# VectorE takes slot 0's logits ahead of the last index score, a weight split and a branch's low part; TensorE computes each slot's logits ahead of a value product

## The chip, the cores and the metric

One core of a Trainium2 chip runs the whole program. The metric is the device time of one execution in microseconds. The engines are TensorE (PE in the rows, PEld for its weight loads), VectorE (DVE), ScalarE (ACT), GpSimd (POOL) and SyncE (SP), whose queue loads the weights.

## The reference, cut to what matters

Two layers over 256 tokens of width 1024. Each has a gated feed-forward block, a mixer of three branches, a cross attention to a memory, and a second feed-forward block.

```python
for l in range(DEPTH):
    x = x + 0.5 * swiglu_ffn(rms_norm(x, ffn1_norm[l]), ffn1_w_gu[l], ffn1_w_down[l])
    h = rms_norm(x, mix_norm[l])
    (x_r, g_r, q_b, c_kv, q_i, k_i, w_i, q_c, k_c, v_c, f_c,
     gate_a, gate_b, gate_c) = jnp.split(h @ w_in[l], _split_points(), axis=-1)
    o_a = rglru_branch(x_r, g_r, ...)
    o_b = dsa_branch(q_b, c_kv, q_i, k_i, w_i, ...)
    o_c = fox_branch(q_c, k_c, v_c, f_c, forget_bias[l])
    merged = (jax.nn.sigmoid(gate_a) * (o_a @ w_branch[l, 0])
              + jax.nn.sigmoid(gate_b) * (o_b @ w_branch[l, 1])
              + jax.nn.sigmoid(gate_c) * (o_c @ w_branch[l, 2]))
    x = x + merged @ w_out[l]
    x = x + memory_cross_attention(...)
    x = x + 0.5 * swiglu_ffn(rms_norm(x, ffn2_norm[l]), ffn2_w_gu[l], ffn2_w_down[l])
```

Branch a is a gated linear recurrence. Branch c is causal attention with 8 heads of 64 and a bias that grows with distance (a cumulated forget gate). Branch b is attention over 64 selected keys per query; an index score chooses them: `score = einsum(relu(qi . ki), wi)` over 8 index heads, and the 64 largest of a row are kept.

## The kernel before, in words

**Units.** All weights stream through SBUF in units of 1 MB (`raw`, a ring of three slots). SyncE's queue loads a unit; ScalarE writes its rounded copy `w_hi` in two halves (L509); VectorE writes the remainder `w_lo = raw - w_hi` in two halves (L517). TensorE multiplies three times for each tile (hi by hi, hi by lo, lo by hi). The split of a unit into the two parts is made three units ahead: `splits(..., name)` splits the unit that follows `name` by three in the ring.

**The index stage.** Eight index slots (`for i in range(IDX_SLOTS)`): TensorE makes the dot products of two index heads, ScalarE takes their positive part into `lg[:, i % 2]` (L1005), and VectorE adds them to `score` with two multiply-adds (L1350, L1352), with the mask at every fourth slot. Behind every second slot stands one unit (`IDX_FILL`: qc0, kc0, qc1, kc1). VectorE also does the recurrence of branch a here, after slot 3. After slot 7 it makes `o_lo[0] = gr - o_hi[0]` (L1370), the low part of branch a's output, which unit ba0 reads in slot 6 of the stream, and then the split that belongs to `IDX_FILL[7]`.

**The stream.** Sixteen attention slots follow, `for s in range(STREAM + 3)`: slots 0 to 7 are branch c, 8 to 15 branch b; a slot is two heads of one block of 128 queries. The block is `(s % 8) // 4`, so slots 0 to 3 and 8 to 11 have 128 keys and the others 256. The work of one slot is spread over three turns of the loop, and each turn ends with one unit, `FILL[s]`: vc0, vc1, qb0, qb1, ga0, ga1, ba0, ga2, ga3, ba1, gc0, gc1, bc0, gc2, gc3, bc1, gb0, gb1, mk0. Each engine has this order written out by hand, and semaphores join them.

TensorE in turn s: transposes of the probabilities of slot s-1 (L1758, waits for GpSimd's `p_ready`); value product of slot s-2 (L1767, waits for the copy of the transposes and in slot 2 for the copies of vc0 and vc1); logits of slot s (L1779); `kb` in turns 2 and 3, `vb` in turn 8, four transposes of the memory in turns 13 to 16 (L1798); then the unit.

ScalarE in turn s: copy of the transposes of s-1 (L816), copy of the value product of s-2 (L1027), two half splits for `FILL[s-1]` (L509), exponentials of slot s (L1035, waits for VectorE's `lg_ready`), copies and gates of the unit (L816, L897).

VectorE in turn s: logits of s times scale plus bias and their minimum (L1386 and L1391, or L1395; L1398, `lg_ready`); the first half split for `FILL[s-1]` (L517; none in turn 0); reciprocal of the sums (L1403, waits for ScalarE's `exp_ready`); low part of the value product of s-2 (L1409); the second half split; in turns 0 to 7 two rounds of eight maxima of `score` (L1417, L1419); in turns with a unit ba, bc or bb, its merge with the gate (L1234, or L1238 and L1241), which frees the two PSUM halves that the unit used.

GpSimd in turn s: `lg` times the reciprocal (L777, `p_ready`), in turns 1 to 3 a mask (L731), from turn 7 on a bias with the mask for branch b (L743).

`Plan.mix` numbers the jobs in TensorE's order and hands out the four PSUM banks in turn; the logits have banks of their own (`acc_job`), so their place in the order moves no other job to another bank.

Of the kernel before, what the change touches and what calls it, by code (L numbers as in the profile page):

```python
# [21 lines left out]
F32 = mybir.dt.float32  # L22
F32R = mybir.dt.float32r
ACT = mybir.ActivationFunctionType
ALU = mybir.AluOpType
# [76 lines left out]
class Plan:  # L102
# [57 lines left out]
    def mix(self):  # L160
# [22 lines left out]
        for s in range(STREAM + 3):  # L183
            if 0 <= s - 1 < STREAM:
                self.job(("pt", s - 1))
            if 0 <= s - 2 < STREAM:
                self.job(("pv", s - 2))
            if s < STREAM:
                self.acc_job(("qk", s))
            if s in (2, 3):  # L190
                self.job(("kb", s - 2))
            if s == 8:
                self.job(("vb", 0))
                self.job(("vb", 1))
            if 13 <= s < 17:
                self.job(("mt", s - 13))
            self.w_unit(FILL[s])
# [46 lines left out]
def block_kernel(nc, t, out):  # L244

    ctx = ExitStack()
    with ctx:
# [880 lines left out]
        def _(v):  # L1128
# [127 lines left out]
            for l in range(DEPTH):  # L1256
# [83 lines left out]
                splits(v, split_lo, l, "qi1")  # L1340
                for i in range(IDX_SLOTS):
                    blk, h, base, m = idx_slot_of(i)
# [11 lines left out]
                    if i % 4 == 3:  # L1354
                        mask = chunked[:, SEQ - s_len:SEQ]
                        v.tensor_tensor(sc, sc, mask, ALU.add)
                        v.drain()
                    v.drain().then_inc(score_step, 1)
                    if i == 3:
                        v.wait_ge(rg_sqrt, l + 1)  # L1360
# [6 lines left out]
                        v.drain().then_inc(rg_h, 1)  # L1367
                    if i == 7:
                        v.wait_ge(oa_ready, l * 1 + 1)
                        v.tensor_tensor(o_lo[0][:], gr[:], o_hi[0][:].bitcast(F32), ALU.subtract)  # L1370
                        v.drain().then_inc(oa_lo_ready, 1)
                    if i in IDX_FILL:
                        splits(v, split_lo, l, IDX_FILL[i])

                for s in range(STREAM + 3):
                    if s < STREAM:
# [21 lines left out]
                        v.tensor_reduce(nm[:, s % 2, :], lgs, AX_X, ALU.min).then_inc(lg_ready, 1)  # L1398
                    if s >= 1:
                        splits(v, split_lo, l, FILL[s - 1], (0,))  # L1400
                    if s < STREAM:
                        v.wait_ge(exp_ready, l * STREAM + s + 1)
                        v.reciprocal(ri[:, s % 2, :], sm[:, s % 2, :]).then_inc(ri_ready, 1)  # L1403
                    if 0 <= s - 2 < STREAM:
# [5 lines left out]
                                        ALU.subtract).then_inc(bank_of(("pv", k)), 1)  # L1410
                    if s >= 1:
                        splits(v, split_lo, l, FILL[s - 1], (1,))
                    if s < 8:
# [79 lines left out]
        def _(pe):  # L1493
# [194 lines left out]
            for l in range(DEPTH):  # L1688
# [60 lines left out]
                for s in range(STREAM + 3):  # L1749
                    if 0 <= s - 1 < STREAM:  # L1750
# [4 lines left out]
                        for j in range(2):  # L1755
                            for c in range(n_s):
                                col = (j * n_s + c) * P
                                mm = pe.transpose(ps(("pt", k))[:, col:col + P], lg[:, k % 2, j, c * P:c * P + P], ident[:])  # L1758
                        mm.then_inc(job_done, 1)
                    if 0 <= s - 2 < STREAM:  # L1760
                        k = s - 2
# [3 lines left out]
                        for c in range(blk + 1):  # L1765
                            for j in range(2):
                                mm = pe.matmul(ps(("pv", k))[HD * j:HD * j + HD, 0:P],  # L1767
                                               values[:, c, (2 * pr + j) * HD:(2 * pr + j + 1) * HD],
                                               pt[:, k % 2, j, c, :], start=(c == 0), stop=(c == blk))
                        mm.then_inc(job_done, 1)  # L1770
                    if s < STREAM:
                        blk, pr = slot_of(s)
                        s_len = P * (blk + 1)
                        queries, keys = (qc, kc) if s < 8 else (qb, k_b)
                        wait_jobs(pe, l, [f"qc{pr // 2}", f"kc{pr // 2}"] if s < 8 else [f"qb{pr // 2}", ("kb", pr // 2)])
                        if s >= 2:
                            pe.wait_ge(lg_ready, l * STREAM + s - 1)
                        for j in range(2):
                            mm = pe.matmul(logits(s)[:, j, :], queries[HD * j:HD * j + HD, pr, blk * P:blk * P + P],  # L1779
                                           keys[HD * j:HD * j + HD, pr, 0:s_len], start=True, stop=True)  # L1780
                        mm.then_inc(job_done, 1)
# [86 lines left out]
```

## Time and profile before

| | us |
|---|---|
| median of 3 runs | 1404.04 |
| lowest, highest | 1403.73, 1405.26 |
| the profiled execution, its own time | 1402.98 |
| its span | 1401.1 |
| TensorE busy | 1359.5 (97%) |
| VectorE busy | 948.0 (68%) |
| ScalarE busy | 777.6 (56%) |
| GpSimd busy | 130.4 (9%) |

The span is the time from the first to the last instruction of the profiled execution. The share of busy time is a mean over all stages; the gaps of an engine are read in the timeline. The granted clock is 1.00 at 2.4 GHz and 0.50 at 1.2 GHz.

### The profile page before, as it was taken

To read this page: it belongs to the slowest core of one execution; us is meant where nothing else is said; L and a number is where in the kernel's file an instruction comes from. 1 tells how busy PE (TensorE), PEld (TensorE's weight loads), DVE (VectorE), ACT (ScalarE), POOL (GpSimd) and SP (SyncE) were. 2 spreads that over 40 slices of the span, in tenths; PEclk is the share of its full clock that TensorE was granted. 3 is DMA by queue.
4 is the path that set the end of the run, shared out by engine and by line. 5 is a ranking of instruction groups with operands and counts; after the bars stand their busy time and mean duration, and the time that the engine had idled before them with its cause. 6 is when DMAs were issued, how large, how long until landed. Compare 5 with 4: busy or idle time off the path is not lost.

```text
span 1401.1 us, 23740 instructions
## 1 busy us (share of the span) xinstructions
PE 1359.5 (97%) x8802; PEld 1211.1 (86%) x8802; DVE 948.0 (68%) x1456; ACT 777.6 (56%) x1378; POOL 130.4 (9%) x219
## 2 busy tenths in 40 slices
PE   6999999999999999999999999999999999999997
PEld 5888879988899988888888888898989989888886
DVE  5666656879666566666676666668777666666665
ACT  5554545845654565554565555576546446655544
POOL 4010000022320110000010000000224001100000
PEclk9999999999999999999999999999999999999999
DMA  8677664544545546666666667456344554466662
GB/s 241 187 209 210 186 194 151 170 136 154 174 136 185 191 121 181 188 196 187 179 182 194 194 180 213 138 169 191 121 156 146 163 198 151 140 191 186 198 186 75
DMA packets 286384, 243.38 MB, mean 174 GB/s; under 512 B 14344, under 2 KB 263608, under 8 KB 286304
## 3 DMA queue, kind: packets, MB, share of 16 engines
q1 hardware_dynamic: 284176, 236.77, 55.9%
q10 hardware_dynamic: 1600, 4.25, 0.9%
q0 software_dynamic: 528, 1.26, 0.5%
q8 instruction: 54, 0.88, 0.3%
q14 instruction: 26, 0.21, 0.0%
HBM read 241.18 MB, written 1.27 MB: 173 GB/s over the span
## 4 chain that ended last, share of the span: by engine, by line
issue 64%; PE 23%; ACT 4%; DVE 3%; POOL 2%; DVEq 2%; POOLq 1%; DMA 1%; ACTq 0%
PE work L1550 14%; PE work L1625 2%; PE work L1572 2%; ACT w_hi L509 1%; PE acc L1587 1%; PE work L1629 1%; DVE w_lo L517 1%; POOL diag L723 1%; PE acc L1501 1%; PE acc L1779 1%; DVE score L1352 1%; POOLq L722 1%; PE work L1767 1%; ACT lg L1035 1%; DVEq L1353 1%
## 5 line engine op out<-in xcount | busy, mean ns | idle before, releaser
L517 DVE TENSOR_TENSOR w_lo<-raw,w_hi 128x1024 fp32r<-128x1024 f32 x444 | 552.8, 1265 | 100.2 <-ACT w_hi L509 98.7
L509 ACT ACTIVATE w_hi<-raw 128x1024 fp32r<-128x1024 f32 (+1 forms) x442 | 450.9, 1053 | 24.5 <-PE acc L1587 24.5
L1625 PE MATMUL work<-act,w_hi 128*128 128x512 f32 x1408 | 441.4, 395 | 9.8 <-DVE w_lo L517 5.8
L1629 PEld LDWEIGHTS work<-act,w_lo 128*128 128x128 f32 x1408 | 265.5, 189 | 60.5
L1550 PE MATMUL work<-act,w_hi 128*128 128x256 f32 x1664 | 299.1, 281 | 5.3 <-DVE merged L1241 2.5
L1629 PE MATMUL work<-act,w_lo 128*128 128x256 f32 x1408 | 278.4, 279 | 0.0
L1550 PEld LDWEIGHTS work<-act,w_hi 128*128 128x128 f32 x1664 | 255.3, 188 | 13.4 <-issue 5.4
L1550 PE MATMUL work<-act,w_lo 128*128 128x256 f32 x832 | 230.7, 277 | 0.0
L1625 PEld LDWEIGHTS work<-act,w_hi 128*128 128x128 f32 x1408 | 215.4, 188 | 13.6 <-issue 10.6
L823 ACT ACTIVATE gu_s<-work 128x256 f32<-128x256 f32 x176 | 57.9, 381 | 200.8 <-PE work L1629 200.8
L1550 PEld LDWEIGHTS work<-act,w_lo 128*128 128x128 f32 x832 | 156.3, 188 | 0.6 <-issue 0.5
L1161 DVE TENSOR_TENSOR gu_s<-gu_s,work 128x256 f32<-128x256 f32 x176 | 66.2, 418 | 130.1 <-ACT gu_s L823 130.1
L1587 PE MATMUL acc<-w_hi,h_lo 128*128 128x512 f32 x320 | 126.0, 394 | 0.0
L1587 PE MATMUL acc<-w_lo,h_hi 128*128 128x512 f32 x320 | 125.4, 392 | 0.0
L1587 PE MATMUL acc<-w_hi,h_hi 128*128 128x512 f32 x320 | 124.2, 388 | 0.0
L833 ACT ACTIVATE h_hi<-h_f 128x256 fp32r<-128x256 f32 x80 | 33.4, 418 | 102.2 <-PE acc L1587 86.4
L714 POOL TENSOR_TENSOR ms<-ssq 128x1 f32<-128x1 f32 x22 | 5.2, 235 | 878.3 <-ACT junk L798 878.3
L1587 PEld LDWEIGHTS acc<-w_lo,h_hi 128*128 128x128 f32 x320 | 60.1, 188 | 12.3
L1587 PEld LDWEIGHTS acc<-w_hi,h_lo 128*128 128x128 f32 x320 | 60.2, 188 | 11.9
L1587 PEld LDWEIGHTS acc<-w_hi,h_hi 128*128 128x128 f32 x320 | 60.1, 188 | 11.8
L1180 DVE TENSOR_TENSOR h_lo<-h_f,h_hi 128x256 fp32r<-128x256 f32 x80 | 33.8, 423 | 49.2 <-ACT h_hi L833 49.2
L1550 PE MATMUL work<-o_hi,w_hi 128*128 128x256 f32 x192 | 53.8, 280 | 0.0
(240 smaller groups left out, 1726.8 us busy)
## 6 DMA issues: line engine op xcount, KB each, us to landing
raw<-in_ffn_w_gu SPq DMA_DIRECT2D x174, 512.0 KB, 5.0
raw<-in_w_in SPq DMA_DIRECT2D x52, 1024.0 KB, 5.2
raw<-in_ffn_w_down SPq DMA_DIRECT2D x44, 1024.0 KB, 4.9
raw<-in_w_branch SPq DMA_DIRECT2D x12, 1024.0 KB, 5.0
raw<-in_w_mkv SPq DMA_DIRECT2D x8, 1024.0 KB, 5.3
raw<-in_w_out SPq DMA_DIRECT2D x8, 1024.0 KB, 4.9
raw<-in_w_mq SPq DMA_DIRECT2D x4, 1024.0 KB, 5.2
raw<-in_w_mo SPq DMA_DIRECT2D x4, 1024.0 KB, 4.9
```

Of the source, the lines that this page charges most:

```text
L509: eng.activation(halves(w_hi, slot, kind, part), halves(raw, slot, kind, part), ACT.Copy)\
L517: eng.tensor_tensor(halves(w_lo, slot, kind, part), halves(raw, slot, kind, part), halves(w_hi, slot, kind, part).bitcast(F32), ALU.subtra ...
L722: g.drain()
L823: a.activation(gu_s[:, c, g, :], work[:, 2 * c + g, SEQ:2 * SEQ], ACT.Copy).then_inc(cross_ready, 1)
L833: a.activation(dst[:, c, :], h_f[:, c, :], ACT.Copy).then_inc(h_hi_ready, 1)
L1161: v.tensor_tensor(gu_s[:, c, g, :], gu_s[:, c, g, :], work[:, 2 * c + g, 0:SEQ], ALU.add)\
L1180: v.tensor_tensor(lo[:, c, :], h_f[:, c, :], hi[:, c, :].bitcast(F32), ALU.subtract)\
L1550: mm = pe.matmul(out_ps, ww[:, slot, first:first + width], xx[:, k, :], start=(k == 0 and n == 0), stop=(k == kn - 1 and n == 2))
L1572: mm = pe.matmul(out_ps(tt), xx[:, k, tt * P:tt * P + P], ww[:, slot, k * 256 + cols[0]:k * 256 + cols[1]], start=(k == 0 and n == 0), sto ...
L1587: mm = pe.matmul(acc[:, tt, nh * 512:nh * 512 + 512], xx[:, k0 + kk, tt * P:tt * P + P], ww[:, slot, kk * D + nh * 512:kk * D + nh * 512 + ...
L1625: pe.matmul(work[:, 2 * c + g, :], w_hi[:, slot, at_w:at_w + P], act[:, :, k, :], start=(k == 0), stop=False, skip_group_check=True)
L1629: mm = pe.matmul(work[:, 2 * c + g, 0:SEQ], w_lo[:, slot, at_w:at_w + P], act_hi[:, k, :], start=False, stop=(k == KT - 1), skip_group_che ...
```

## The change

On VectorE the last index score (slot 7) goes behind the logits and the minimum of slot 0 of the stream. The split that stood behind it goes into turn 0 in two halves: one ahead of the reciprocal of slot 0, one behind it. The low part of branch a's output goes behind the second half. On TensorE the logits of slot s go ahead of the value product of slot s-2 in every turn. ScalarE and GpSimd keep their order, and so do the loads.

```diff
@@ Plan.mix
             if 0 <= s - 1 < STREAM:
                 self.job(("pt", s - 1))
+            if s < STREAM:
+                self.acc_job(("qk", s))
             if 0 <= s - 2 < STREAM:
                 self.job(("pv", s - 2))
-            if s < STREAM:
-                self.acc_job(("qk", s))
@@ vector
-                for i in range(IDX_SLOTS):
+                def index_scores(i):
                     blk, h, base, m = idx_slot_of(i)
...
+                for i in range(IDX_SLOTS - 1):
+                    index_scores(i)
                     if i == 3:
...
-                    if i == 7:
-                        v.wait_ge(oa_ready, l * 1 + 1)
-                        v.tensor_tensor(o_lo[0][:], gr[:], o_hi[0][:].bitcast(F32), ALU.subtract)
-                        v.drain().then_inc(oa_lo_ready, 1)
                     if i in IDX_FILL:
                         splits(v, split_lo, l, IDX_FILL[i])
...
-                    if s >= 1:
-                        splits(v, split_lo, l, FILL[s - 1], (0,))
+                    if s == 0:
+                        index_scores(IDX_SLOTS - 1)
+                    ahead = FILL[s - 1] if s else IDX_FILL[IDX_SLOTS - 1]
+                    splits(v, split_lo, l, ahead, (0,))
                     if s < STREAM:
                         v.wait_ge(exp_ready, l * STREAM + s + 1)
                         v.reciprocal(ri[:, s % 2, :], sm[:, s % 2, :]).then_inc(ri_ready, 1)
...
-                    if s >= 1:
-                        splits(v, split_lo, l, FILL[s - 1], (1,))
+                    splits(v, split_lo, l, ahead, (1,))
+                    if s == 0:
+                        v.wait_ge(oa_ready, l * 1 + 1)
+                        v.tensor_tensor(o_lo[0][:], gr[:], o_hi[0][:].bitcast(F32), ALU.subtract)
+                        v.drain().then_inc(oa_lo_ready, 1)
@@ tensor
                         mm.then_inc(job_done, 1)
+                    if s < STREAM:
+                        blk, pr = slot_of(s)
+                        s_len = P * (blk + 1)
+                        queries, keys = (qc, kc) if s < 8 else (qb, k_b)
+                        wait_jobs(pe, l, [f"qc{pr // 2}", f"kc{pr // 2}"] if s < 8 else [f"qb{pr // 2}", ("kb", pr // 2)])
+                        if s >= 2:
+                            pe.wait_ge(lg_ready, l * STREAM + s - 1)
+                        for j in range(2):
+                            mm = pe.matmul(logits(s)[:, j, :], queries[HD * j:HD * j + HD, pr, blk * P:blk * P + P],
+                                           keys[HD * j:HD * j + HD, pr, 0:s_len], start=True, stop=True)
+                        mm.then_inc(job_done, 1)
                     if 0 <= s - 2 < STREAM:
                         k = s - 2
                         blk, pr = slot_of(k)
...
-                        mm.then_inc(job_done, 1)
-                    if s < STREAM:
-                        blk, pr = slot_of(s)
-                        s_len = P * (blk + 1)
-                        queries, keys = (qc, kc) if s < 8 else (qb, k_b)
...
```

VectorE, from index slot 6 to slot 0's maxima, before (`score` is the index score, `w_lo` a weight split, `o_lo` the low part, `lg` and `nm` slot 0's logits and their minimum; x4 are slots 6 and 7 together):

```order
L1352 SCALAR_TENSOR_TENSOR score<-lg,wi,score 128x256 x4
L1356 TENSOR_TENSOR score<-score,chunked 128x256
L1370 TENSOR_TENSOR o_lo_70<-gr,o_hi_69 128x1024
L517 TENSOR_TENSOR w_lo<-raw,w_hi 128x1024 x2
L1386 SCALAR_TENSOR_TENSOR lg<-acc,fox_bias 128x2x128
L1391 TENSOR_TENSOR lg<-lg,causal 128x2x128
L1398 TENSOR_REDUCE nm<-lg 128x2
L1403 RECIPROCAL ri<-sm 128x2
```

The same place in the changed kernel:

```order
L1352 SCALAR_TENSOR_TENSOR score<-lg,wi,score 128x256 x2
L1385 SCALAR_TENSOR_TENSOR lg<-acc,fox_bias 128x2x128
L1390 TENSOR_TENSOR lg<-lg,causal 128x2x128
L1397 TENSOR_REDUCE nm<-lg 128x2
L1352 SCALAR_TENSOR_TENSOR score<-lg,wi,score 128x256 x2
L1356 TENSOR_TENSOR score<-score,chunked 128x256
L517 TENSOR_TENSOR w_lo<-raw,w_hi 128x1024
L1404 RECIPROCAL ri<-sm 128x2
L517 TENSOR_TENSOR w_lo<-raw,w_hi 128x1024
L1415 TENSOR_TENSOR o_lo_70<-gr,o_hi_69 128x1024
```

The logits moved ahead of slot 7's scores; the split is in two pieces around the reciprocal, and the low part stands behind them, ahead of the maxima.

TensorE at the head of turn 6, before: transposes of slot 5, the value product of slot 4 (`pt,vc`), the logits of slot 6 (`kc,qc`), then the first product of unit ba0.

```order
L1758 MATMUL work<-ident,lg 128x128 x4
L1767 MATMUL work<-pt,vc 64x128 x4
L1779 MATMUL acc<-kc,qc 128x256 x2
L1550 MATMUL work<-o_hi_69,w_hi 128x256
```

The same place in the changed kernel:

```order
L1762 MATMUL work<-ident,lg 128x128 x4
L1772 MATMUL acc<-kc,qc 128x256 x2
L1782 MATMUL work<-pt,vc 64x128 x4
L1554 MATMUL work<-o_hi_69,w_hi 128x256
```

The value product and the logits have changed places; what stands ahead of and behind the two is as before.

## Rows read from the trace of the kernel before

**Rows 1.** Waits of TensorE: line, for whom, us in total, times, longest.

```profile
PE work L1758 <- POOL lg L777: 5.6, 2, 2.8
...
PE work L1550 <- DVE merged L1241: 2.5, 4, 0.6
```

**Rows 2.** Windows, TensorE: us, busy (count), granted clock, DMA share, GB/s.

```profile
292.50:295.90 3.40, 3.40 (x18) 0.50 0.00 1
978.60:985.40 6.80, 6.32 (x29) 0.50 0.30 98
```

**Rows 3.** Timeline, TensorE, layer 0: start, us, engine, line, operation, [idle before].

```profile
282.41 0.39 PE L1572 MATMUL work<-w_hi,act 128*128 128x256 f32 x1
...
288.05 0.28 PE L1572 MATMUL work<-w_hi,act 128*128 128x256 f32 x1
291.13 0.44 PE L1758 MATMUL work<-ident,lg 128*128 128x128 f32 x2 [2.80 <-POOL lg L777]
291.50 0.49 PE L1779 MATMUL acc<-kc,qc 64*128 64x128 f32 x4
...
299.21 0.38 PE L1758 MATMUL work<-ident,lg 128*128 128x128 f32 x2
300.14 0.44 PE L1767 MATMUL work<-pt,vc 128*64 128x128 f32 x4 [0.56 <-ACT vc L816]
```

**Rows 4.** Timeline, TensorE, layer 1, slots 0 and 1.

```profile
979.08 0.69 PE L1758 MATMUL work<-ident,lg 128*128 128x128 f32 x2 [2.77 <-POOL lg L777]
...
988.40 0.38 PE L1758 MATMUL work<-ident,lg 128*128 128x128 f32 x2
```

**Rows 5.** Timeline, VectorE, layer 0, slots 0 and 1.

```profile
282.51 1.05 DVE L1352 SCALAR_TENSOR_TENSOR score<-lg,wi,score 128x256 f32<-128x256 f32 x2 [0.17 <-issue]
...
284.22 1.23 DVE L1370 TENSOR_TENSOR o_lo<-gr,o_hi 128x1024 fp32r<-128x1024 f32 x1 [0.17 <-issue]
285.57 2.36 DVE L517 TENSOR_TENSOR w_lo<-raw,w_hi 128x1024 fp32r<-128x1024 f32 x2
287.85 0.42 DVE L1386 SCALAR_TENSOR_TENSOR lg<-acc,fox_bias 128x256 f32<-128x256 f32 x1
...
290.22 0.17 DVE L1403 RECIPROCAL ri<-sm 128x2 f32<-128x2 f32 x1 [0.95 <-ACT lg L1035]
...
292.04 0.42 DVE L1386 SCALAR_TENSOR_TENSOR lg<-acc,fox_bias 128x256 f32<-128x256 f32 x1 [0.24 <-PE acc L1779]
```

**Rows 6.** Timeline, ScalarE, layer 0, slot 0.

```profile
284.60 1.28 ACT L1035 ACT_TABLE_LOAD   x1
289.31 0.40 ACT L1035 ACTIVATE lg<-lg,nm 128x128 f32<-128x128 f32 x1 [3.42 <-DVE nm L1398]
```

**Rows 7.** Timeline, GpSimd beside VectorE, layer 0.

```profile
259.38 1.36 POOL L731 TENSOR_TENSOR fox_bias<-fox_bias,causal 128x256 f32<-128x256 f32 x1 [16.06 <-DMA fox_bias<-cum_dram]
...
260.06 2.90 DVE L517 TENSOR_TENSOR w_lo<-raw,w_hi 128x1024 fp32r<-128x1024 f32 x2
...
294.68 0.17 DVE L1403 RECIPROCAL ri<-sm 128x2 f32<-128x2 f32 x1
...
294.92 1.51 POOL L777 TENSOR_TENSOR lg<-lg,ri 128x256 f32<-128x256 f32 x1 [3.85 <-DVE ri L1403]
```

**Rows 8.** Timeline, three engines, layer 0, slots 6 and 7.

```profile
329.40 0.66 PE L1767 MATMUL work<-pt,vc 128*64 128x128 f32 x8
...
329.98 0.70 PE L1779 MATMUL acc<-kc,qc 64*128 64x256 f32 x4
...
330.10 0.28 ACT L1027 ACTIVATE o_hi<-work 128x128 fp32r<-128x128 f32 x1
...
332.22 0.51 ACT L1035 ACTIVATE lg<-lg,nm 128x256 f32<-128x256 f32 x1
...
337.81 1.29 DVE L1234 SCALAR_TENSOR_TENSOR merged<-gate,work 128x512 f32<-128x512 f32 x2
...
338.56 0.39 PE L1550 MATMUL work<-act,w_hi 128*128 128x256 f32 x1 [0.54 <-DVE merged L1234]
```

More of the change, by code:

```diff
@@ L1769, in _ @@
                                                pt[:, k % 2, j, c, :], start=(c == 0), stop=(c == blk))
-                        mm.then_inc(job_done, 1)
-                    if s < STREAM:
-                        blk, pr = slot_of(s)
-                        s_len = P * (blk + 1)
-                        queries, keys = (qc, kc) if s < 8 else (qb, k_b)
[L1775 to L1780, printed above, removed]
                         mm.then_inc(job_done, 1)
```

## The prediction

> **What bounds the kernel now.** I read the waits of TensorE first: the engine is busy nearly throughout, so only its gaps and its clock can give time back. Two kinds of wait matter here. Both waits for GpSimd's normalised probabilities (5.6 us, two times) stand ahead of slot 0's transposes, once per layer, and four waits of about 0.6 us are for a merge by VectorE [rows 1]. Then I read the granted clock: after the first of the long waits it is 0.50 for the whole of 292.5 to 295.9, and around the second it is 0.50 from 978.6 to 985.4 [rows 2]. So a long wait costs its own length and a stretch at 1.2 instead of 2.4 GHz behind it.
>
> TensorE's rows in layer 0: unit vc0 runs from 282.41 to 288.05 + 0.28 = 288.33, that is 5.92 us; the transposes of slot 0 start at 291.13 after 2.80 us idle; those of slot 1 at 299.21; the value product of slot 0 at 300.14 waits 0.56 us for ScalarE's copy of vc1 [rows 3]. From slot 0's transposes to slot 1's it takes 8.08 us there, and 988.40 - 979.08 = 9.32 us in layer 1 [rows 3, 4]. At the full clock it would be 0.37 (transposes to logits, 291.13 to 291.50) + 0.42 (the logits; their row has 0.49, its end modelled) + 5.92 = 6.71 us. The low clock therefore costs 1.37 us in layer 0 and 2.61 us in layer 1.
>
> Why slot 0 is late is in VectorE's rows: slot 0's logits are ready when vc0 starts (282.41), but VectorE does the last index score at 282.51, the branch's low part at 284.22, both halves of a weight split at 285.57 and only at 287.85 the logits; the reciprocal comes at 290.22 [rows 3, 5]. Nothing waits for the three pieces ahead of it at that moment.
>
> **The change, part by part.**
>
> *Slot 0 on VectorE.* No instruction is added or removed. The step 282.51 is now slot 0's logits, say 282.55. ScalarE's exponentials begin as the minimum is there, 289.31 - 287.85 = 1.46 us after the logits' start [rows 5, 6], so the minimum is at 284.01, and VectorE itself is free at about 283.95. Then the last index score takes 284.22 - 282.51 = 1.71 us, to 285.66, and half of the pair of splits (287.85 - 285.57) / 2 = 1.14 us, to 286.80 [rows 5]. ScalarE is not ready at 284.01: its table load runs from 284.60 to 285.88 [rows 6]. The exponentials then need 290.22 - 289.31 = 0.91 us to the reciprocal [rows 5, 6]: 286.79. Both arms meet, and the reciprocal is at 286.80.
>
> Behind it VectorE starts the other half split at once. This is how slot 1 runs now: reciprocal at 294.68, GpSimd's product from 294.92 and 1.51 us long, so 1.75 us from reciprocal to probabilities [rows 7]. I take 1.75 us: 288.55, and the transposes at 288.61. TensorE arrives at 288.33. The stall falls from 2.80 to 0.28 us in layer 0 and, the rows of layer 1 having the same shape (2.77 [rows 4]), to about 0.27 there: 2.52 + 2.50 = 5.02 us. The low clock behind the stall should go too: 1.37 + 2.61 = 3.98 us. That takes a gap of 0.3 us as harmless, as those of 0.56 us [rows 3] are.
>
> The Trainium skill, page "SBUF — State Buffer", section "Who interferes with whom", speaks against this placing: a VectorE instruction with both inputs in SBUF and a GpSimd instruction that reads SBUF exclude each other, and the one issued second waits for the whole of the first. The 1.51 us row agrees with it; were there no such exclusion, the sum would be at most 0.28 us per layer better, 6.7 us and not 6.1.
>
> *Slot 1 pays for it.* The low part (1.35 us from 284.22 to 285.57, with its drain [rows 5]) now stands behind the second half split: 286.88 + 1.14 = 288.02. GpSimd's product slips between the two: at 259.38 a GpSimd instruction lasted 1.36 us between two long ones of VectorE and the pair of splits behind took 2.90 us and not 2.36 [rows 5, 7], so VectorE waits 0.54 us. The low part ends at 289.9. The two rounds of maxima run from 290.30 (0.08 behind the reciprocal) to 292.04 - 0.24 = 291.80 now [rows 5], 1.50 us: so slot 1's logits start at 291.4 and not 292.04, 0.64 us earlier, while TensorE is 2.5 us earlier. Reciprocal 2.64 us later (294.68 - 292.04, partly ScalarE's), then 1.75 us: probabilities at 295.8. TensorE arrives at 288.61 + 6.71 = 295.32. That is 0.5 us; where ScalarE is not in the way it is 0.3. I take 0.4 us a layer: -0.8 us.
>
> *Logits ahead of the value product, slot 2.* The 0.56 us wait at 300.14 [rows 3] is covered by slot 2's logits (0.42) and by the stall just counted: +0.56 twice, 1.12 us.
>
> *The same exchange in the other slots.* VectorE gets its logits 0.4 to 0.6 us earlier, but the value product ends later by the logits' length, and ScalarE copies that product before it does two half splits, and only then the exponentials. Slot 6 shows it: value product 329.40, logits 329.98 with 0.70, ScalarE's copy at 330.10, then without a gap the splits and the exponentials at 332.22 [rows 8]. With the logits first the value product starts about 0.6 us later, the copy too, and the exponentials, and VectorE cannot take its reciprocal before. In most slots this is hidden: probabilities are ready ahead of TensorE (slot 1 now: 294.92 + 1.51 = 296.43 against 299.21, of which 1.37 is the slow clock, so 1.4 us in hand [rows 3, 7]). But behind slot 6 VectorE goes without a pause to the merge at 337.81, and TensorE's next unit waits for it, 0.54 us at 338.56 [rows 8]. That wait grows by 0.6 us. The other merges that TensorE waits for are those of bc0 and bc1 (slots 12 and 15), the four waits in [rows 1]. Slot 15 has slot 6's shape: 0.6 us. In slot 12 the value product is half as long and ScalarE is itself late: between 0 and 0.6, I choose 0.4. Together 1.6 us a layer, -3.2 us; the bounds are 0 (the earlier logits make up for it) and 0.7 (the logits' whole row) at each of six places, 4.2 us.
>
> **Sum.** 5.02 + 3.98 - 0.8 + 1.12 - 3.2 = 6.1 us gained. The profiled execution took 1402.98 us (span 1401.1), 1.06 us less than the median of the runs, 1404.04. From the median: 1397.9, say 1398.0 us. Weight loads should follow: a split moves by under 1 us, and its unit is used two units of 6 us later.
>
> **Rivals.**
> 1. The exchange is free, as the earlier logits let VectorE catch up at the merges: 9.3 us gained, 1394.7. For it: VectorE waits for logits in many slots. Against: the exponentials follow ScalarE's splits in slot 6 [rows 8]. Chance 0.2.
> 2. GpSimd does not get in between the split and the low part, and waits for both: probabilities 1.14 to 1.35 us later, of which slot 1's 0.4 comes back; 0.8 us a layer, 1399.6. For it: VectorE's next long instruction is there at once. Against: the row at 259.38 [rows 7]. Were the clock to fall again as well, 0.5 us would be left. Chance 0.08.
> 3. The longer stalls at the merges bring the clock down there: 1.37 to 2.61 us each, one a layer, 4 us: 1402. For it: at bc1's merge two waits lie close together. Against: single gaps of 0.54 and 0.56 us do not do it. Chance 0.12.
> 4. Slower: ScalarE's lateness of 0.5 us reaches the transposes in all of slots 3 to 15, and not only three merges: 13 x 0.5 x 2 = 13 us against 9.3 gained, 1407.7. It decides where probabilities are less than 0.6 us ahead of TensorE; slot 1 has 1.4 us. Chance 0.05.
> 5. The edit at slot 0 does nothing: another wait, ScalarE's table load or GpSimd, holds the transposes as long; then only 1.12 - 3.2, that is 1406.1. Chance 0.03.
>
> The forecast has 0.52. **Range and chances.** 1393.0 (rival 1, with slot 1's stall gone too) to 1402.0 (rival 3) leaves rivals 4 and 5 and the tails out. About 0.2% (2.8 us) is what a measurement of this kernel can tell from no change: faster is below 1401.2, slower above 1406.8. Faster: 0.52, 0.2, 0.08 and a third of rival 3: 0.84. Within: most of rivals 3 and 5: 0.11. Slower: rival 4: 0.05.
>
> **What the changed kernel's profile would show.** TensorE waits under 0.6 us for slot 0's transposes, and the granted clock stays at its upper level there. The reciprocal of slot 0 is about 3.4 us earlier against unit vc0, GpSimd's product there lasts about 1.5 us, and slot 1's transposes wait some 0.4 us. The wait for vc1's copy is gone. The waits for merges go from about 0.6 to about 1.1 us in both layers; if they stay at 0.6 or vanish, my price of the exchange was wrong. I am wrong altogether if transposes in slots 2 to 15 wait, or if slot 0's wait stays over 2 us.

## The result and the profile after

The changed kernel takes 1395.74 us (median of 6 runs, 1393.06 to 1397.28) and the kernel before 1404.19 us (6 runs, 1402.01 to 1405.26). The ratio is 0.9944, 95% interval 0.9934 to 0.9954: 7.9 us less, 6.5 to 9.3. The forecast was 6.1 us less. Timed once more in a later series (below), the same kernel came to 0.9969 (0.9956 to 0.9982), 4.4 us less. The two intervals do not overlap, so a difference of 2 us between two kernels of this case is taken as shown only with a trace behind it. The profiled execution of the changed kernel took 1396.78 us (span 1394.9), that of the kernel before 1402.98.

The waits of TensorE in the changed kernel, which answer to [rows 1] (line, for whom, us in total, times, longest):

```profile
PE work L1554 <- DVE merged L1234: 2.2, 2, 1.1
...
PE work L1802 <- DVE merged L1241: 1.5, 2, 0.7
PE work L1554 <- DVE merged L1241: 1.3, 2, 0.6
PE work L1762 <- POOL lg L777: 1.2, 4, 0.3
```

The wait for GpSimd's probabilities fell from 5.6 us in two pieces to 1.2 us in four; the waits for merges grew. The windows around slot 0's transposes, which answer to [rows 2] (us, busy, granted clock, DMA share, GB/s):

```profile
288.20:291.00 2.80, 2.54 (x20) 1.00 0.63 174
291.00:296.00 5.00, 4.68 (x40) 1.00 0.32 112
974.70:982.00 7.30, 6.78 (x55) 1.00 0.47 144
```

The granted clock is 1.00 behind both, where it was 0.50 for 3.4 us and for 6.8 us. VectorE's timeline in slots 0 and 1, layer 0, which answers to [rows 5]:

```profile
282.35 0.42 DVE L1385 SCALAR_TENSOR_TENSOR lg<-acc,fox_bias 128x256 f32<-128x256 f32 x1 [0.39 <-PE acc L1772]
...
286.64 0.17 DVE L1404 RECIPROCAL ri<-sm 128x2 f32<-128x2 f32 x1
286.73 1.21 DVE L517 TENSOR_TENSOR w_lo<-raw,w_hi 128x1024 fp32r<-128x1024 f32 x1
287.85 1.63 DVE L1415 TENSOR_TENSOR o_lo<-gr,o_hi 128x1024 fp32r<-128x1024 f32 x1
...
291.22 0.42 DVE L1385 SCALAR_TENSOR_TENSOR lg<-acc,fox_bias 128x256 f32<-128x256 f32 x1
```

GpSimd beside it, which answers to [rows 7]:

```profile
286.89 1.52 POOL L777 TENSOR_TENSOR lg<-lg,ri 128x256 f32<-128x256 f32 x1 [26.51 <-DVE ri L1404]
```

The reciprocal is 4.29 us after the logits' start, and the probabilities are ready at 288.41. The low part lasts 1.63 us and not 1.23: GpSimd's product got in ahead of it. TensorE in the same stretch and behind slots 6 and 15, which answers to [rows 3, 8]:

```profile
288.46 0.44 PE L1762 MATMUL work<-ident,lg 128*128 128x128 f32 x2 [0.30 <-POOL lg L777]
...
295.49 0.44 PE L1762 MATMUL work<-ident,lg 128*128 128x128 f32 x2 [0.32 <-POOL lg L777]
...
335.04 0.39 PE L1554 MATMUL work<-act,w_hi 128*128 128x256 f32 x1 [1.12 <-DVE merged L1234]
...
402.31 0.63 PE L1802 MATMUL work<-ident,mem_x 128*128 128x128 f32 x4 [0.74 <-DVE merged L1241]
403.58 0.38 PE L1554 MATMUL work<-act,w_hi 128*128 128x256 f32 x1 [0.65 <-DVE merged L1241]
```

Slot 2's wait for vc1's copy is gone, the wait behind slot 6 went from 0.54 to 1.12 us, and there is none behind slot 12. From slot 0's to slot 1's transposes it is 7.03 us (8.08 and 9.32 before). Why the merges are late shows in three engines in slot 6 (start, us, engine):

```profile
325.94 0.66 PE L1782 MATMUL work<-pt,vc 128*64 128x128 f32 x8
...
326.64 0.28 ACT L1027 ACTIVATE o_hi<-work 128x128 fp32r<-128x128 f32 x1 [0.58 <-PE work L1782]
...
328.71 0.50 ACT L1035 ACTIVATE lg<-lg,nm 128x256 f32<-128x256 f32 x1
...
334.30 1.28 DVE L1234 SCALAR_TENSOR_TENSOR merged<-gate,work 128x512 f32<-128x512 f32 x2
```

ScalarE now stands 0.58 us for the value product, where it went on without a gap before [rows 8]; in VectorE's rows of the same slot the reciprocal now waits 0.27 us for the exponentials, where it did not wait before.

### The profile page after: what moved, and what is told of

It reads as the page before. It is cut to its first block, busy times and chain, and to the rows that moved or that the text cites. A ratio compares the mean times of both kernels' runs of the same rounds, so it can differ in the third digit from the quotient of the medians.

```text
span 1394.9 us, 23740 instructions
## 1 busy us (share of the span) xinstructions
PE 1357.8 (97%) x8802; PEld 1208.2 (87%) x8802; DVE 945.5 (68%) x1456; ACT 780.3 (56%) x1378; POOL 134.6 (10%) x219
## 4 chain that ended last, share of the span: by engine, by line
issue 63%; PE 27%; ACT 3%; DVE 2%; POOL 2%; POOLq 1%; DMA 1%; DVEq 0%; ACTq 0%; SPq 0%
PE work L1554 17%; PE work L1629 3%; PE work L1633 1%; PE acc L1591 1%; PE acc L1772 1%; ACT w_hi L509 1%; PE work L1782 1%; PE work L1576 1%; POOL diag L723 1%; PE work L1762 1%; DVE w_lo L517 1%; PE acc L1505 1%; PE work L1748 0%; POOLq L722 0%; DMA rows_dram<-brow_dram 0%
## 5 line engine op out<-in xcount | busy, mean ns | idle before, releaser
L777 POOL TENSOR_TENSOR lg<-lg,ri 128x256 f32<-128x256 f32 (+1 forms) x32 | 36.7, 1147 | 200.2 <-DVE ri L1404 200.2
```

The costliest lines, as they stand in the source:

```text
L777: g.tensor_tensor(lg[:, s % 2, :, 0:s_len], lg[:, s % 2, :, 0:s_len], ri[:, s % 2, :].unsqueeze(2).to_broadcast([P, 2, s_len]), ALU.mult)\
```

## The experiments

The theory in test has three parts: VectorE's edit carries the whole gain, by a shorter stall and by the clock; the exchange on TensorE costs through ScalarE's queue; and slot 1 pays a little for the low part. The rivals: the exchange carries part of the gain; VectorE's own work makes the merges late. Ratios are to runs of the kernel before beside them. The table's first row is a series of its own; rows 2 to 5, rows 6 to 8 and rows 9 to 12 are three more, each on one chip.

| kernel | median us | ratio | 95% interval |
|---|---|---|---|
| changed kernel | 1395.74 | 0.9944 | 0.9934 to 0.9954 |
| VectorE's edit alone | 1395.48 | 0.9946 | 0.9932 to 0.9960 |
| exchange alone | 1407.42 | 1.0025 | 1.0013 to 1.0036 |
| low part in turn 2 | 1397.29 | 0.9956 | 0.9942 to 0.9970 |
| no exchange in turns 6, 15 | 1396.46 | 0.9953 | 0.9939 to 0.9967 |
| ScalarE's split first | 1392.99 | 0.9923 | 0.9906 to 0.9940 |
| low part in turn 2, exchange in turn 2 alone | 1393.78 | 0.9931 | 0.9914 to 0.9947 |
| low part ahead of the reciprocal | 1400.58 | 0.9978 | 0.9968 to 0.9989 |
| changed kernel again | 1398.03 | 0.9969 | 0.9956 to 0.9982 |
| split first, low part in turn 2 | 1393.17 | 0.9929 | 0.9912 to 0.9945 |
| the same without the exchange | 1394.84 | 0.9938 | 0.9922 to 0.9954 |
| exchange alone again | 1406.26 | 1.0023 | 1.0013 to 1.0034 |

### VectorE's edit alone

```diff
@@ against the changed kernel: Plan.mix, and the same two blocks on TensorE
-            if s < STREAM:
-                self.acc_job(("qk", s))
             if 0 <= s - 2 < STREAM:
                 self.job(("pv", s - 2))
+            if s < STREAM:
+                self.acc_job(("qk", s))
```

> Only VectorE's edit is made; TensorE keeps the value product ahead of the logits. My theory: the whole gain of the change is VectorE's edit, the exchange is a small net loss. The stall ahead of slot 0's transposes is 0.3 us, that of slot 1 0.3 us, slot 2's value product waits 0.2 to 0.6 us for vc1's copy, and the waits for merges are those of the kernel before (0.54, 0.6, 0.25 + 0.65 us a layer). No low clock at slot 0. 8.5 us less than before, that is as fast as the changed kernel or up to 1 us faster. Rival (the exchange carries part of the gain): 5 to 7 us less than before.

0.9946, 7.6 us less (5.6 to 9.5). The same gain as the whole change within the interval. TensorE's timeline of this kernel in layer 0:

```profile
288.26 0.44 PE L1762 MATMUL work<-ident,lg 128*128 128x128 f32 x2 [0.30 <-POOL lg L777]
...
295.29 0.44 PE L1762 MATMUL work<-ident,lg 128*128 128x128 f32 x2 [0.53 <-POOL lg L777]
...
334.27 0.39 PE L1554 MATMUL work<-act,w_hi 128*128 128x256 f32 x1 [0.55 <-DVE merged L1234]
...
401.33 0.63 PE L1802 MATMUL work<-ident,mem_x 128*128 128x128 f32 x4 [0.25 <-DVE merged L1241]
```

The merge waits of this layer are those of the kernel before, to 0.01 us; in layer 1 the one behind slot 12 is 0.42 us, as in the second trace of the kernel before. Slot 1's transposes wait 0.53 us here and 0.33 us in layer 1. Slot 2's value product does not wait in this trace, where I had 0.2 to 0.6 us: slot 1's own wait covers vc1's copy. The interval of the time reaches into the rival's 5 to 7 us; what speaks against the rival is the exchange alone, next.

### The exchange alone, twice

```diff
@@ against the kernel before: Plan.mix, and the same two blocks on TensorE
+            if s < STREAM:
+                self.acc_job(("qk", s))
             if 0 <= s - 2 < STREAM:
                 self.job(("pv", s - 2))
-            if s < STREAM:
-                self.acc_job(("qk", s))
```

> Only the exchange on TensorE is made; VectorE keeps its order. My theory: slot 0 still stalls 2.8 us with the low clock behind it; slot 2's wait of 0.56 us goes, slot 6's merge wait grows from 0.54 to 1.1 us, slot 15's from 0.25 + 0.65 to 0.75 + 0.65 us, slot 12's goes either way. Within 1.5 us of the kernel before. Rival (the exchange is a gain): 2 us or more less than before.

1.0025, 3.5 us slower (1.8 to 5.1), where I had within 1.5. The profiled execution was one of the quickest, 1402.89 us: the low clock is missing at layer 0's slot 0, and the merge waits are 1.13 us behind slot 6 in layer 0 alone, none behind slot 12, and 0.75 + 0.64 us behind slot 15, 3.9 us in all against 4.1 in the kernel before. So it was run again:

> The exchange alone once more, since it came out 3.5 us slower than the kernel before where its trace showed no such loss. Theory (the waits at the merges grow by 0.6 and 0.5 us and the one behind slot 12 goes either way; the speed of the pairs and the clock belong to the single execution): 0 to 2 us more than the kernel before. Rival (the exchange alone brings the slow pairs or the low clock more often): 3 to 4 us more again.

1.0023 again, 3.2 us: outside the theory's 0 to 2, and the rival's size. TensorE's waits in the second trace of it:

```profile
PE work L1758 <- POOL lg L777: 5.5, 2, 2.8
...
PE work L1550 <- DVE merged L1241: 2.6, 4, 0.6
PE work L1550 <- DVE merged L1234: 2.2, 2, 1.1
PE work L1798 <- DVE merged L1241: 2.2, 4, 0.7
```

and in the second trace of the kernel before, of the same form:

```profile
PE work L1758 <- POOL lg L777: 5.5, 2, 2.8
...
PE work L1550 <- DVE merged L1241: 2.1, 4, 0.6
PE work L1767 <- ACT vc L816: 1.1, 2, 0.6
PE work L1550 <- DVE merged L1234: 1.1, 2, 0.5
...
PE work L1798 <- DVE merged L1241: 0.5, 2, 0.2
```

Merges and vc1's copy together are 7.0 us against 4.8: the exchange loses 2.2 us in waits, the forecast's own price for it (3.2 lost, 1.1 gained). Some 1 us of the measured 3.4 (the mean of the two) is not in these waits and stays open. The rival's cause, a low clock more often, may be part of it in the second series and is not in the first: the mean granted clock of the runs was 0.9925 against 0.9924 of the kernel before in the first series, and 0.9911 against 0.9926 in the second.

### The low part in turn 2

```diff
-                    if s == 0:
+                    if s == 2:
                         v.wait_ge(oa_ready, l * 1 + 1)
                         v.tensor_tensor(o_lo[0][:], gr[:], o_hi[0][:].bitcast(F32), ALU.subtract)
```

> The changed kernel with the low part of branch a in turn 2 of the stream in place of turn 0. My theory: slot 1's transposes no longer wait (0.32 us a layer in the changed kernel), slot 0's wait stays 0.3 us; slot 2's wait for vc1's copy comes back in part (0.1 to 0.2 us). 0.3 to 0.7 us less than the changed kernel. Rival (GpSimd, which had the low part in its way, is the one that gains): slot 0's wait falls too.

In the trace slot 1's transposes do not wait any more and slot 0's wait is 0.30 us, as the theory has it; nothing waits in slot 2 either, where I had 0.1 to 0.2 us. The time does not show the 0.6 us: 0.9956 lies between the two results of the changed kernel.

In layer 0 of this trace the wait behind slot 6 is gone too; in layer 1 it is 1.12 us. What differs ahead of the two merges is above all who got in first, GpSimd's product or VectorE's half split; layer 0, then layer 1:

```profile
329.84 2.14 POOL L777 TENSOR_TENSOR lg<-lg,ri 128x512 f32<-128x512 f32 x1 [5.41 <-DVE ri L1404]
329.86 1.22 DVE L517 TENSOR_TENSOR w_lo<-raw,w_hi 128x1024 fp32r<-128x1024 f32 x1
...
1015.22 1.04 POOL L777 TENSOR_TENSOR lg<-lg,ri 128x512 f32<-128x512 f32 x1 [6.29 <-DVE ri L1404]
1015.25 2.10 DVE L517 TENSOR_TENSOR w_lo<-raw,w_hi 128x1024 fp32r<-128x1024 f32 x1
```

The second run of the changed kernel, below, comes back to this.

### No exchange in turns 6 and 15

```diff
+def logits_first(s):
+
+    return s not in (6, 15)
...
+                    for kind in ("qk", "pv") if logits_first(s) else ("pv", "qk"):
```

> The changed kernel with the logits ahead of the value product in all turns but 6 and 15. My theory (the exchange makes ScalarE's copy, splits and exponentials late, and with them VectorE's merge): the wait behind slot 6 falls from 1.12 to 0.5 to 1.0 us (turns 4 and 5 still carry part of the lateness), that behind slot 15 from 0.74 to 0.25 us; 1.0 to 2.1 us less than the changed kernel. Rival (VectorE's own work makes the merge late): both waits stay.

Waits of this kernel in layer 0:

```profile
335.24 0.39 PE L1560 MATMUL work<-act,w_hi 128*128 128x256 f32 x1 [0.88 <-DVE merged L1240]
...
378.86 0.63 PE L1809 MATMUL work<-ident,mem_x 128*128 128x128 f32 x4 [0.34 <-DVE merged L1247]
380.13 0.38 PE L1560 MATMUL work<-act,w_hi 128*128 128x256 f32 x1 [0.64 <-DVE merged L1247]
...
402.54 0.63 PE L1809 MATMUL work<-ident,mem_x 128*128 128x128 f32 x4 [0.25 <-DVE merged L1247]
```

Behind slot 15 the wait is back at 0.25 us and behind slot 6 it fell to 0.88, in both layers, both inside the theory's values: the exchange made them. That the 0.34 us left behind slot 6 come from the turns ahead of it is argued, not shown. Behind slot 12 0.34 + 0.64 = 0.98 us came up, which the first trace of the changed kernel did not have. The time (0.9953) shows no gain over the changed kernel's first result, where I had 1.0 to 2.1 us; against its second, whose trace has the same 0.98 us, it is 2.2 us less.

### ScalarE's half split ahead of its copy

```diff
@@ scalar
+                    if s >= 1:
+                        splits(a, split_hi, l, FILL[s - 1], (0,))
                     if 0 <= s - 2 < STREAM:
                         k = s - 2
                         blk, pr = slot_of(k)
                         wait_done(a, l, ("pv", k))
...
                     if s >= 1:
-                        splits(a, split_hi, l, FILL[s - 1])
+                        splits(a, split_hi, l, FILL[s - 1], (1,))
```

> The changed kernel, but ScalarE does the first half split of a turn ahead of its copy of the value product and the second behind it, so that it no longer stands idle for the product that now ends later. My theory (the merge waits grew because ScalarE stood behind the later value product): the wait behind slot 6 falls from 1.12 to about 0.5 us and that behind slot 15 from 0.74 to 0.25 us in both layers, with the logits still first everywhere. Rival (VectorE's own work, or the earlier logits, makes the merges late): they stay at 1.1 and 0.74. By the time: 1 to 2 us less than the changed kernel, which its own spread may hide.

ScalarE's copy of the value product in slot 6, and TensorE's waits, in layer 0, with the logits first in every turn:

```profile
326.25 0.28 ACT L1029 ACTIVATE o_hi<-work 128x128 fp32r<-128x128 f32 x1
...
333.70 0.39 PE L1556 MATMUL work<-act,w_hi 128*128 128x256 f32 x1 [0.42 <-DVE merged L1236]
...
400.70 0.63 PE L1804 MATMUL work<-ident,mem_x 128*128 128x128 f32 x4 [0.17 <-DVE merged L1243]
```

The copy does not wait any more (0.58 us in the changed kernel). The waits are 0.42 and 0.17 us in both layers, against 1.12 and 0.74 in the changed kernel and 0.54 and 0.25 before. Behind slots 6 and 15 GpSimd gets in first here as in the changed kernel's first trace, so that is not what changed. Taking ScalarE's wait for the value product away is enough: that wait was the cause, and the rival falls, since VectorE's work is unchanged. Now the earlier logits even gain 0.1 us at each of these two places; behind slot 12 the wait is 0.61 us. 0.9923: 10.8 us less than the kernel before, and 3 or 6.5 us less than the two results of the changed kernel, where I had 1 to 2: more than the waits of the traces account for. It is the best version by its ratio; the interval clears that of the second timing of the changed kernel and overlaps that of the first.

### One exchange only

```diff
+    return s == 2
...
-                    if s == 0:
+                    if s == 2:
                         v.wait_ge(oa_ready, l * 1 + 1)
```

> VectorE's edit with the low part in turn 2, and the logits ahead of the value product in turn 2 alone. My theory: every stall has its smallest value at once: slot 0 at 0.3 us, slots 1 and 2 none, merges 0.54, 0 or 0.6, and 0.25 + 0.65 us. 1 us less than VectorE's edit alone. Rival (the low part in turn 2 delays slot 2's chain): a wait at slot 2's transposes.

0.9931. Slot 0 waits 0.31 us, slots 1 and 2 not at all, and the merges 0.55, 0.42, 0.25 and 0.65 us. The theory's waits, to 0.2 us. It is 2.1 us below VectorE's edit alone (0.9946), where I had 1; the two intervals overlap, so that difference is not shown.

### The low part ahead of the reciprocal

```diff
                     splits(v, split_lo, l, ahead, (0,))
+                    if s == 0:
+                        v.wait_ge(oa_ready, l * 1 + 1)
+                        v.tensor_tensor(o_lo[0][:], gr[:], o_hi[0][:].bitcast(F32), ALU.subtract)
+                        v.drain().then_inc(oa_lo_ready, 1)
                     if s < STREAM:
                         v.wait_ge(exp_ready, l * STREAM + s + 1)
...
-                    if s == 0:
-                        v.wait_ge(oa_ready, l * 1 + 1)
-                        v.tensor_tensor(o_lo[0][:], gr[:], o_hi[0][:].bitcast(F32), ALU.subtract)
-                        v.drain().then_inc(oa_lo_ready, 1)
```

> The changed kernel with the low part ahead of slot 0's reciprocal, which makes the stall ahead of slot 0's transposes longer by its 1.35 us: 1.6 us where the kernel before had 2.8 and the changed one has 0.3; slot 1 should not wait. It asks from which length on a stall brings the clock down. Theory A (the clock falls with the long stalls only): no low clock at slot 0, 2.0 to 2.7 us more than the changed kernel. Rival B (1.6 us is long enough): the granted clock is 0.50 behind it for 3.4 us or more, 5 to 8 us more than the changed kernel.

The stall, and the windows behind it in both layers:

```profile
289.20 0.44 PE L1762 MATMUL work<-ident,lg 128*128 128x128 f32 x2 [1.55 <-POOL lg L777]
...
295.75 0.38 PE L1762 MATMUL work<-ident,lg 128*128 128x128 f32 x2
```

```profile
289.20:296.00 6.80, 6.80 (x56) 1.00 0.53 166
976.80:983.00 6.20, 6.20 (x52) 1.00 0.65 179
```

The clock stayed up behind 1.55 and 1.52 us in this execution, which is theory A, and slot 1 does not wait. The time decides less: by the ratios it is 4.8 us above the changed kernel's first result and 1.3 us above its second, where A had 2.0 to 2.7 and B 5 to 8. The mean granted clock of its 12 runs is 0.9942, against 0.9965 and 0.9953 in the two series of the changed kernel and 0.9914 in the kernel before beside it; so the clock may fall at slot 0 in some of its other executions, which no trace shows.

### The kernel before, again

No edit.

> The kernel before once more, for a second trace of it. In its first trace the stretch from the last merge wait to the third transposes (406.9 to 477.2, and 1096.5 to 1166.8) took 70.3 us in both layers, while four other kernels with the same instructions there took 72.0 us in most layers. If the speed of TensorE's pairs there belongs to the single execution, 72.0 us can come up here too; if the exchange makes it slow, it is 70.3 us again in both layers. The stalls at slot 0 are 2.8 us again.

72.0 us came up, in the very kernel that had 70.3: TensorE's windows from 410 to 470, first of this trace, then of the first trace of the kernel before (us, busy, matmuls, granted clock):

```profile
410.00:470.00 60.00, 60.00 (x420) 1.00 0.54 180
```

```profile
410.00:470.00 60.00, 60.00 (x434) 1.00 0.56 189
```

420 and 434 matmuls in 60 us, the same instructions at the same granted clock. The whole stretch has 516 matmul records in either trace, in 72.0 and in 70.3 us, so it is not a matter of missing records. In the 14 traces of this case, two stretches each, it took 70.3 us 7 times and 72.0 us 21 times, and the 70.3 came up with and without the exchange. So this belongs to the execution; why is open. The stalls at slot 0 were 2.78 and 2.76 us again.

### The changed kernel, again

No edit.

> The changed kernel once more, timed beside its variants on one chip, and with a second trace. Theory: 0.993 to 0.996 of the kernel before. Stalls as in its first trace: 0.3 us at slots 0 and 1, 1.12 us behind slot 6, 0.74 + 0.65 us behind slot 15; behind slot 12 it is 0 or about 1 us, as GpSimd or VectorE gets in first there.

0.9969. Behind slot 12 it waits 0.34 + 0.64 us this time. What differs stands in slot 12, GpSimd's product beside VectorE's half split; first trace, then the second:

```profile
374.71 2.14 POOL L777 TENSOR_TENSOR lg<-lg,ri 128x512 f32<-128x512 f32 x1 [4.25 <-DVE ri L1404]
374.73 1.22 DVE L517 TENSOR_TENSOR w_lo<-raw,w_hi 128x1024 fp32r<-128x1024 f32 x1
```

```profile
374.60 1.04 POOL L777 TENSOR_TENSOR lg<-lg,ri 128x512 f32<-128x512 f32 x1 [4.14 <-DVE ri L1404]
374.62 2.10 DVE L517 TENSOR_TENSOR w_lo<-raw,w_hi 128x1024 fp32r<-128x1024 f32 x1
```

Both start 0.02 us apart. In the first, GpSimd takes 1.1 us longer and VectorE goes on at once, so the merge is early; in the second VectorE stands 0.9 us. In slot 15 of the second trace it went in VectorE's favour in both layers and left only 0.62 us of wait there.

In the slots ahead of the three merges it is the exchange that opens this. Slots 6, 12 and 15 of both layers in the 14 traces are 84 such pairs. In 54 of them VectorE stood less than 0.6 us for the exponentials ahead of its reciprocal, and GpSimd got in first every time; all 30 pairs of the five traces without the exchange in these slots (the kernel before twice, VectorE's edit alone, one exchange only, the split first without the exchange) are among them. In the other 30, all with the exchange, VectorE stood 0.70 us, and it got in first in 12: there the merge wait is gone behind slots 6 and 12, and 0.62 us behind slot 15. So ScalarE's lateness costs a longer wait or, by chance, takes one away.

### Split first, with and without the exchange

```diff
@@ both, against the variant with ScalarE's split first
-                    if s == 0:
+                    if s == 2:
                         v.wait_ge(oa_ready, l * 1 + 1)
@@ the second alone: Plan.mix, and the same two blocks on TensorE
-            if s < STREAM:
-                self.acc_job(("qk", s))
             if 0 <= s - 2 < STREAM:
                 self.job(("pv", s - 2))
+            if s < STREAM:
+                self.acc_job(("qk", s))
```

> The changed kernel with ScalarE's first half split ahead of its copy of the value product, and the low part in turn 2. Theory: as the variant with the split first (stalls of 0.4, 0.6 and 0.2 + 0.6 us at the merges), and slot 1's wait of 0.31 us gone: 0.6 us less than that variant, about 0.992 of the kernel before. Rival: slot 2's chain, now behind the low part, waits and gives it back.

> VectorE's edit with the low part in turn 2 and ScalarE's first half split ahead of its copy, but the value product ahead of the logits as in the kernel before. It asks whether the exchange is worth anything once ScalarE does not wait for it. Theory: merge waits as in the kernel before (0.54, 0.6 or 0, 0.25 + 0.65 us), slot 2's value product waits about 0.5 us for vc1's copy. 0.5 to 1.5 us more than the same with the logits first. Rival (the exchange is worth nothing or costs): the same time or less.

0.9929 with the exchange and 0.9938 without. The first has no wait in slots 1 and 2; the second waits 0.56 us in slot 2 for vc1's copy in both layers. That is 1.1 us in the traces and 1.7 us in the medians, inside the intervals, so the worth of the exchange here is shown by the waits and not by the time. The first is not faster than the split alone (0.9923), where I had 0.6 us less: slot 1's wait is under what can be measured.

## Why the prediction was right, and where it was not

**Slot 0.** The forecast had the reciprocal at 286.80 and a stall of 0.28 us; the trace has 286.64 and 0.30. Both arms met there as worked out: VectorE's half split ended at 286.61, and ScalarE's last row of exponentials too, its table load having ended at 285.71. GpSimd's product lasted 1.52 us, as in [rows 7]. In slot 2 of the same trace the same pair went the other way:

```profile
299.98 0.61 POOL L777 TENSOR_TENSOR lg<-lg,ri 128x256 f32<-128x256 f32 x1 [3.86 <-DVE ri L1404]
300.00 1.67 DVE L517 TENSOR_TENSOR w_lo<-raw,w_hi 128x1024 fp32r<-128x1024 f32 x1
```

The rule of the Trainium skill, page "SBUF — State Buffer", section "Who interferes with whom", agrees with both placings: whichever of the two gets in first holds the other up. Behind the half split the product took 1.52 us and not 0.61; behind the product the half split took 1.67 us and not 1.21.

**The clock.** No low clock at slot 0 in any of the ten traces with VectorE's edit; in the four traces without it (the kernel before twice, the exchange twice) it was 0.50 in one layer at least. The price of 3.98 us holds for the first trace of the kernel before. It differs between places and executions: with stalls of 2.8 us the low stretch was 3.4 us at one place and 6.8 at another, and in the second trace of the same kernel it took 8.09 us from slot 0's to slot 1's transposes in both layers, not 8.08 and 9.32. Over all runs the mean granted clock lies between 0.9942 and 0.9970 in the ten series with VectorE's edit, and between 0.9911 and 0.9926 in the two of the exchange alone and the three of the kernel before beside them, so the gain in clock is not one of single executions. (For the kernel before in the first series the clock of each run is not known.)

**Slot 1.** 0.32 us against 0.4. The variant with the low part ahead of the reciprocal, where slot 1 does not wait, has 295.75 - 289.20 = 6.55 us from slot 0's to slot 1's transposes at the full clock. The forecast's 6.71 was built from rows whose ends are modelled and is 0.16 us too long: the low clock cost 0.16 us a layer more than I had, and slot 1's wait costs 0.48 us by the time and not 0.32. The two cancel in the sum.

**Slot 2.** The wait went, 0.56 us a layer. VectorE's edit alone did the same in both layers, by slot 1's own wait; the exchange earns it only where slot 1 does not wait, as the last pair of variants shows.

**The exchange elsewhere.** Behind slot 6 it went from 0.54 to 1.12 us (forecast 1.14), behind slot 15 from 0.25 to 0.74 (0.85). ScalarE's queue is shown as the cause by moving one half split. In slot 12 I chose a growth of 0.4 us, and the wait vanished in the first trace and was 0.98 us (forecast 1.01) in the second: what I did not see is that two engines start there 0.02 us apart, and that the exchange makes either of them come first. This term, 2 x 1.0 us, is what was mis-sized in the first trace: 1.2 us saved in place of 0.8 lost. In the second trace it was slot 15 that gained: 0.62 us of wait, where 0.90 had been and 1.50 was forecast.

**The sum.** Forecast 6.1 us less; measured 7.9 and 4.4, a mean of 6.2. The waits in the first pair of traces: 2.50 - 0.32 + 0.56 - 0.58 + 0.61 - 0.49 = 2.28 us a layer, 4.6 for both, and 4.0 for the clock: 8.5 in all. Its profiled execution is only 6.2 us shorter: 1.7 us went back where layer 0's stretch of 70.3 us took 72.0, and the remaining 0.6 us in smaller pieces that I did not follow. The second traces of both kernels, summed the same way, give 4.94 (slot 0's stall), 2.12 (from slot 0's to slot 1's transposes, clock and slot 1's wait together), 1.12 (slot 2), -1.15, -1.12 and +0.54 (slots 6, 12 and 15): 6.45 us, where the two executions are 8.0 apart. So the mechanism and the terms are borne out, but that the mean of two timings falls on the forecast to 0.1 us is luck: the two are 3.5 us apart, and who gets in first, the speed of the stretch and the low clock elsewhere each move an execution by 1 us or more. The range's lower end was also added up wrong: rival 1 with slot 1's stall gone is 1393.9, not 1393.0.

Rival 1 (the exchange is free) is out: it costs 2.2 us in waits and 3.4 us by the time when alone. Rival 2 (GpSimd overtaken twice) is out by the low part's 1.63 us. Rival 3 (the clock falls at the merges) showed in no trace. Rival 4 (slower) is out: no transposes in slots 2 to 15 wait in either trace of the changed kernel. Rival 5 (no effect at slot 0) is out by the stall of 0.30 us.

## What to carry to other kernels

Read what an engine does between the arrival of its input and its answer: three pieces that nobody needed yet stood ahead of slot 0's logits, and the stall they made was paid twice, in waiting and in clock. When two steps change places on one engine, follow both results through the queue of the next engine: a copy that stands ahead of urgent work makes that work as late as its own input. A loss found that way is mended by the order of the waiting engine, here one half split moved, and not by undoing the exchange.

## What the runs showed of the hardware that was not expected

- The same matmuls at the same granted clock run at two speeds: 434 or 420 of them in 60 us, 70.3 or 72.0 us for a stretch, in one kernel from one execution to the next. Two such stretches make up to 3.4 us of a run. The spread also goes with the clock: of 52 runs of the kernel before, the 18 with a mean granted clock of 0.989 or 0.990 took 1405.1 us on average, and the 6 with 0.996 or 0.997 took 1400.2.
- Where GpSimd's product is recorded 0.02 or 0.03 us ahead of VectorE's half split, either of them can be the one that gets in first, and the other then takes 0.9 to 1.1 us longer. In slots with such a pair on the path, traces of one kernel differ by 1 us. In slots 6, 12 and 15 VectorE got in first in 12 of 30 pairs after it had stood 0.70 us, and in none of 54 where it had stood less than 0.6 us; in slot 5 it got in first 5 times without any stand, so the stand alone does not decide. What decides is open.
- The length of a stall alone does not decide whether a low clock follows. It stayed up behind 1.55 and 1.52 us. Behind the same 2.35 us at layer 1's first norm it fell in 9 of the 14 traces (in the kernel before it was 0.50 from 893.2) and stayed up in 5. Behind 3.25 us at layer 0's first norm it stayed up in 2 (the exchange alone, and the split first with the low part in turn 2), and behind 2.59 us ahead of slot 0 in the exchange alone it stayed up too.
